# Attention scores and values as three fp32r passes, with the small work of the attention stages put in another order

## The chip, the cores and the metric

The program runs on one core of one Trainium2 chip. The metric is the device time in microseconds (us), the median of three runs. Five engines of the core take part, each with its own queue of instructions that it works off in order: TensorE (PE in the profile), VectorE (DVE), ScalarE (ACT), GpSimd (POOL) and SyncE (SP), which here only starts DMAs. They meet by semaphores: an instruction waits until a counter has reached a number.

## The reference

One layer of a hybrid decoder for 1024 prompt tokens (`x_prompt`) and 32 sample tokens (8 sequences of 4). All three branches read one normed input through one matrix of 4608 columns:

```python
h = _rmsnorm(x, norm_g)
proj = jnp.einsum('btd,de->bte', h, w_in)
qa, ka, va, ga, xb, gb, qc, kc, vc, gc = jnp.split(proj, SPLIT_IDX, axis=-1)
...
qc = _rmsnorm(qc.reshape(B, T, SWA_HEADS, SWA_HEAD_DIM), q_g)
kc = _rmsnorm(kc.reshape(B, T, SWA_KV_HEADS, SWA_HEAD_DIM), k_g)
...
mixed = jnp.concatenate([oa * jax.nn.silu(ga), ob * jax.nn.silu(gb), oc * jax.nn.silu(gc)], axis=-1)
y = x + jnp.einsum('bte,ed->btd', mixed, w_out)
```

`oa` is a retention, `ob` a gated linear recurrence, `oc` the attention that the change touches: 4 query heads of 128 on 2 key/value heads, a window of 128 keys, so that each block of 128 queries reads its own and the previous block of keys:

```python
s = jnp.einsum('bnqhgd,bnkhd->bnhgqk', q.astype(f32), k.astype(f32)) * (SWA_HEAD_DIM ** -0.5)
s = s - slopes[...] * dist
s = jnp.where(valid[None, :, None, None], s, NEG_INF)
m = jnp.maximum(jnp.max(s, axis=-1, keepdims=True), sink)
p = jnp.exp(s - m)
denom = jnp.sum(p, axis=-1, keepdims=True) + jnp.exp(sink - m)
o = jnp.einsum('bnhgqk,bnkhd->bnqhgd', p / denom, v.astype(f32))
```

## The kernel before

The input projection is cut into 18 units of 256 columns, worked off in the order of `UNITS`. Its products are made in three passes of the type fp32r (`three_pass`, lines 447 to 449): each operand is split into a high part, rounded to fp32r (by ACT), and a low part, the rest (by DVE), and PE multiplies low by high, high by low and high by high. The attention's own products, scores and values, are plain fp32: PE's records hold two for each such matmul.

Units 12 and 14 are `kvC` (keys and values of the first and the second key/value head, called half 0 and half 1), units 13 and 15 `qC` (the two query heads on it), 16 and 17 `gA` (gates). In `kvC` and `qC` a unit has nine groups: eight tiles of 128 tokens (24 passes of 256 columns each on PE) and a ninth for the 32 sample tokens, on which PE spends nothing there: these rows are projected ahead, by `sample_rows`, when the next unit takes them too. Groups of `gA` have 24 passes of 352 columns.

The order of the work is written out by hand. Every engine runs the same program of units and groups. PE does a group in two halves and after each half the *side work* of a half-step s (after the first half of group j it is s = 2j, after the second 2j+1). ACT and DVE do the side work of 2j, then the group's own work, then the side work of 2j+1. `att_slot` maps unit and half-step to the half-step of the attention (unit 13: s, unit 14: s + 18, and so on for half 1), and `att_side` of each engine lists what is done there. For tile t of queries:

- unit 13: PE projects group t, ACT squares and sums it (`q_stat`, line 1045), POOL takes the root (line 1710), DVE scales q (`q_norm`, line 1503)
- half-step 2t+3: PE transposes q (`att_q`, line 680), ACT copies it to `qT` (`q_copy`, line 1067)
- 2t+4: PE makes the scores (line 691), DVE adds the bias and takes the maximum (`att_max`, lines 1531 and 1537); 2t+5: ACT takes the exponentials (`att_exp`, line 1075)
- 2t+6: DVE divides (`att_probs`, lines 1545 and 1547); 2t+8: PE transposes the probabilities (line 704), ACT copies them to `pT` (line 1087)
- 2t+12: PE multiplies by the values (line 714), DVE by the gate (`att_mix`, line 1555)

In `kvC` the same goes for k: `k_stat` (lines 1023 and 1025), `k_norm` (1487), `turn_k` (670), `k_copy` (1032); and ACT copies the sample rows of the next unit out of PSUM (`hold_copy`, line 906). Beside it all ACT and DVE split the next unit's weights (`w_hi`, line 861; `w_low`, line 1249), in `kvC` and `qC` at half-steps 3, 5, 7 and 9 (DVE one later). `SILU_AT` places eight silu rows of 1056 columns on ACT (line 889).

Of the kernel before, what the change touches and what calls it, by code (L numbers as in the profile page):

```python
# [68 lines left out]
def done(g):  # L69
    return sum(UNITS[u][0] not in TOKEN_MAJOR or j < NT for u, j in GROUPS[:g + 1])  # L70

# [34 lines left out]
def layer(nc, io):  # L106
    gammas = [float(1.0 - 2.0 ** (-5.0 - h)) for h in range(H)]
    with ExitStack() as ctx:
# [97 lines left out]
        with ExitStack() as r:  # L206
            sb("mixed_c", [P, 3 * H, TOK], scope=r)
            kT = sb("kT", [P, 2, TOK], scope=r)
            v_c = sb("v_c", [P, 2, NT + 1, DH], scope=r)
# [3 lines left out]
            qT = sb("qT", [P, 2, 2 * P], scope=r)  # L213
            pr = sb("pr", [P, 2, 2, 2 * P + 1], scope=r)
            pT = sb("pT", [P, 2, 4 * P], scope=r)
            cache = sb("cache", [P, DB, DH], scope=r)
            kcT = sb("kcT", [P, DB, P], scope=r)
            tail_rows = pT[0:36, 0, :]
            p_sel = kcT[:, 0:2, :].rearrange("p a n -> p (a n)")
        with ExitStack() as r:  # L220
# [23 lines left out]
            k_ss k_pow kn_set kT_done kT_set q_ss q_pow qn_half qn_set qT_done qT_set  # L244
            sc_done biased sink_set mx_set ex_set pr_set pT_done pT_set av_done mix_c
# [36 lines left out]
        def _(sp):  # L282
# [81 lines left out]
            for half in range(2):  # L364
# [7 lines left out]
                for t in (NT - 1, NT):  # L372
                    n9 = 9 * half + t
                    sp.wait_ge(S_["kn_set"], n9 + 1)
                    if t < NT:
                        store(io["p_k"][:, half], kn[:, n9 % 2, :], "stored_kv")
                        store(io["p_v"][:, half], v_c[:, half, t, :], "stored_kv")
                        continue
                    for b in range(DB):
                        rows = slice(b * DS, (b + 1) * DS)  # L380
                        store(io["s_k"][b, WINDOW - DS:WINDOW, half], kn[rows, n9 % 2, :], "stored_kv")
                        store(io["s_v"][b, WINDOW - DS:WINDOW, half], v_c[rows, half, t, :], "stored_kv")
# [37 lines left out]
        SILU_AT = {(7, 3): 0, (7, 4): 1, (10, 4): 2, (10, 5): 3, (12, 4): 4, (12, 5): 5, (12, 6): 6, (12, 7): 7}  # L420
# [4 lines left out]
        def att_slot(u, s):  # L425

            if u in (13, 15):
# [3 lines left out]
            if u == 16:  # L431
                return 1, s + 18
            if u == 17 and s < 6:
                return 1, s + 30
# [9 lines left out]
        def _(pe):  # L444
# [214 lines left out]
            def turn_k(n9):  # L659
# [4 lines left out]
                if n9 > 0:  # L664
                    pe.wait_ge(S_["kT_set"], n9)
                    if n9 >= 9:
                        pe.wait_ge(S_["qT_set"], 9)
                else:
# [3 lines left out]
            def att_q(n9):  # L672
# [3 lines left out]
                pe.wait_ge(S_["kT_set"], 9 * (n9 // 9) + 9)  # L676
                if n9 > 0:
                    pe.wait_ge(S_["qT_set"], n9)
                for g in range(2):
# [4 lines left out]
            def att_scores(half, t):  # L684
                n8 = 8 * half + t
                pe.wait_ge(S_["qT_set"], 9 * half + t + 1)
                if n8 > 0:
                    pe.wait_ge(S_["biased"], n8)
                for g in range(2):
                    lo = P if t == 0 else 0  # L690
                    mm = pe.matmul(bb[1][:, g * 2 * P + lo:(g + 1) * 2 * P],  # L691
                                   qT[:, (9 * half + t) % 2, g * P:(g + 1) * P],
                                   kT[:, half, (t - 1) * P + lo:(t + 1) * P], start=(g == 0), stop=True,
                                   skip_group_check=True)
                mm.then_inc(S_["sc_done"], 1)

            def att_turn(half, t):
                n8 = 8 * half + t
                pe.wait_ge(S_["pr_set"], n8 + 1)
                if n8 > 0:  # L700
                    pe.wait_ge(S_["pT_set"], n8)
                for kt in range(1 if t == 0 else 0, 2):
# [5 lines left out]
            def att_values(half, t):  # L708
                n8 = 8 * half + t
                pe.wait_ge(S_["pT_set"], n8 + 1)  # L710
                if n8 > 0:
                    pe.wait_ge(S_["mix_c"], n8)
                for kt in range(1 if t == 0 else 0, 2):
                    mm = pe.matmul(bb[3][:, 0:2 * P], v_c[:, half, t - 1 + kt, :],  # L714
                                   pT[:, n8 % 2, kt * 2 * P:(kt + 1) * 2 * P], start=(kt == 0 or t == 0),
                                   stop=(kt == 1))
                mm.then_inc(S_["av_done"], 1)

            def samp_scores(half):
# [4 lines left out]
                for e in range(2):  # L724
                    for c in range(4):
                        b = 2 * c + e
                        q = qT[:, (9 * half + NT) % 2, NS * b:NS * b + NS]
                        pe.matmul(bb[4][32 * c:32 * c + 32, 0:P], q, kcT[:, b, :], start=(e == 0), stop=(e == 1),
                                  skip_group_check=True)
                for e in range(2):  # L730
                    for c in range(4):
                        b = 2 * c + e
                        q = qT[:, (9 * half + NT) % 2, NS * b:NS * b + NS]
                        mm = pe.matmul(bb[4][32 * c:32 * c + 32, P:P + NS], q, kT[:, half, SEQ:TOK], start=False,
# [8 lines left out]
            def samp_values(half):  # L743
# [7 lines left out]
                for c in range(4):  # L751
                    mm = pe.matmul(bb[4][32 * c:32 * c + 32, 2 * P:3 * P], kcT[0:NS, 4, 32 * c:32 * c + 32],
                                   v_c[0:NS, half, NT, :], start=False, stop=True, skip_group_check=True)
# [6 lines left out]
            def att_side(half, s):  # L760
                if s % 2 == 1 and 0 <= (s - 3) // 2 <= NT and s >= 3:
                    att_q(9 * half + (s - 3) // 2)
                if s % 2 == 0 and 0 <= (s - 12) // 2 < NT:
                    att_values(half, (s - 12) // 2)
# [86 lines left out]
        def _(act):  # L851
# [157 lines left out]
            def k_stat(u, j):  # L1009
# [10 lines left out]
                if j == NT:  # L1020
# [4 lines left out]
                act.activation(v_c[0:n, half, j, :], bank[0:n, DH:2 * DH], ACT.Copy,  # L1025
                               scale=rcol[0:n, j:j + 1]).then_inc(S_["k_ss"], 1)

            def k_copy(n9):
# [3 lines left out]
                act.activation(kT[:, half, chunk_cols(t)], bb[0][:, 0:n], ACT.Copy).then_inc(S_["kT_set"], 1)  # L1032
# [16 lines left out]
            def q_copy(n9):  # L1049
                n = tile_rows(n9 % 9)  # L1050
                act.wait_ge(S_["qT_done"], n9 + 1)
                if n9 >= 2:
                    h2, t2 = divmod(n9 - 2, 9)
                    if t2 < NT:
                        act.wait_ge(S_["sc_done"], 8 * h2 + t2 + 1)
                    else:
                        act.wait_ge(S_["ss_done"], h2 + 1)
                if n9 % 9 == NT:
                    act.wait_ge(S_["q_zero"], n9 // 9 + 1)
                    q = qT[:, n9 % 2, :].rearrange("p (c x) -> p c x", c=4)  # L1060
# [6 lines left out]
                act.activation(qT[:, n9 % 2, 0:2 * n], bb[0][:, 0:2 * n], ACT.Copy).then_inc(S_["qT_set"], 1)  # L1067
# [11 lines left out]
            def att_pcopy(half, t):  # L1079
# [4 lines left out]
                if n8 >= 2:  # L1084
                    act.wait_ge(S_["av_done"], n8 - 1)
                lo = 2 * P if t == 0 else 0
                act.activation(pT[:, n8 % 2, lo:], bb[2][:, lo:], ACT.Copy).then_inc(S_["pT_set"], 1)
# [21 lines left out]
            def att_side(half, s):  # L1109
# [4 lines left out]
                if s % 2 == 1 and 0 <= (s - 5) // 2 < NT:  # L1114
                    att_exp(half, (s - 5) // 2)
# [121 lines left out]
        def _(dve):  # L1237
# [236 lines left out]
            def k_norm(u, j):  # L1474
# [9 lines left out]
                if j == NT:  # L1484
                    dve.wait_ge(S_["held"], TOKEN_UNITS.index(u) + 1)
                bank = hold if j == NT else proj_bank(g)
                dve.scalar_tensor_tensor(out=kn[0:n, n9 % 2, :], in0=bank[0:n, 0:DH],
                                         scalar=stat[0:n, 16 + n9 % 2:17 + n9 % 2], in1=gain[0:n, 1, :],
                                         op0=ALU.mult, op1=ALU.mult).then_inc(S_["kn_set"], 1)

# [78 lines left out]
            def samp_qzero(half):  # L1569
                dve.wait_ge(S_["sc_done"], 8 * half + 7)  # L1570
                dve.memset(qT[:, (9 * half + NT) % 2, :], 0.0).then_inc(S_["q_zero"], 1)
# [16 lines left out]
            def att_side(half, s):  # L1588
                if s % 2 == 0 and 0 <= (s - 6) // 2 < NT:
                    att_probs(half, (s - 6) // 2)  # L1590
                if s % 2 == 0 and 0 <= (s - 12) // 2 < NT:
# [3 lines left out]
                if s == 17:  # L1595
                    samp_qzero(half)
                if s == 22:
# [6 lines left out]
            def side(u, s):  # L1604
# [40 lines left out]
                if (u, s) in LRU_AT["scan"]:  # L1645
                    lru_scan(LRU_AT["scan"][u, s])
                if att_slot(u, s):
# [14 lines left out]
            for u in range(1, NU):  # L1662
                for j in range(n_groups(u)):
# [3 lines left out]
                    if UNITS[u][0] == "qC":  # L1667
                        q_norm(u, j)
# [244 lines left out]
```

## Time and profile before

| what | value |
|---|---|
| median of 3 runs | 671.33 us (671.24 to 672.15) |
| the profiled execution | 672.29 us, its span 670.2 us |
| PE busy | 664.5 us, 99% of the span |
| DVE, ACT, POOL busy | 300.2, 288.5, 89.0 us |
| granted TensorE clock | 1.000 |

The span runs from the first to the last instruction; the profiled execution's own time holds 2.1 us more. A matmul's record covers its way through the array and overlaps with its neighbours', so the time that a matmul costs is the distance from its start to that of the next, and not its mean duration. Half 0's attention lies in 373 to 429 us of the span (units 13 and 14), half 1's in 444 to 504 us (units 15 and 16).

### The profile page before, as it was taken

Reading aid. Unit: us, or ns where it says so; the run is one execution under the profiler, and the core shown is the slowest. Engines: PE = TensorE matmul, PEld = TensorE weight load, DVE = VectorE, ACT = ScalarE, POOL = GpSimd, SP = SyncE. Lnnn points to the kernel's source line nnn. Section 1 sums busy time; section 2 is a strip of 40 time slices with the busy share of each in tenths; the row PEclk is TensorE's granted clock in tenths of the full one; section 3 lists DMA queues with packets and bytes.
Section 4 is the critical chain, followed back from the end, with each engine's and each line's share of the span. In section 5 each row is a group of like instructions: output and inputs, shape, how many; then the busy total and the mean of one; then the engine's idle time right before and its main releaser. Section 6 shows DMA issues by size and latency. Waiting matters only on the chain.

```text
span 670.2 us, 12606 instructions
## 1 busy us (share of the span) xinstructions
PE 664.5 (99%) x5030; PEld 646.9 (97%) x5030; DVE 300.2 (45%) x665; ACT 288.5 (43%) x711; POOL 89.0 (13%) x206
## 2 busy tenths in 40 slices
PE   9999999999999999999999999999999999999998
PEld 9999999999999999999999999999899999999998
DVE  6311453443545668695442465237542870400000
ACT  7473343323233377799635555345543460200000
POOL 0001141424342000000003321222100000000000
PEclk9999999999999999999999999999999999999999
DMA  9913105131312301101040202131002551522220
GB/s 347 383 36 96 64 1 202 52 99 33 99 33 72 106 1 63 64 1 64 1 152 2 79 1 80 38 100 64 1 1 74 158 179 34 160 66 66 66 66 32
DMA packets 28149, 54.19 MB, mean 81 GB/s; under 512 B 2520, under 2 KB 20696, under 8 KB 25884
## 3 DMA queue, kind: packets, MB, share of 16 engines
q1 hardware_dynamic: 27804, 52.85, 23.6%
q8 instruction: 40, 0.66, 0.4%
q10 hardware_dynamic: 288, 0.54, 0.2%
q14 instruction: 17, 0.14, 0.1%
HBM read 46.30 MB, written 9.12 MB: 83 GB/s over the span
## 4 chain that ended last, share of the span: by engine, by line
PE 97%; DMA 1%; ACT 1%; issue 1%; POOL 0%; DVE 0%; DVEq 0%; SPq 0%; POOLq 0%
PE proj L447 22%; PE proj L449 21%; PE proj L448 21%; PE branch L449 4%; PE branch L448 4%; PE branch L447 4%; PE branch L714 2%; PE branch L691 2%; PE branch L558 1%; PE branch L575 1%; PE branch L646 1%; PE branch L592 1%; DMA lead<-w_units 1%; PE proj L492 1%; PE proj L497 1%; PE proj L500 1%
## 5 line engine op out<-in xcount | busy, mean ns | idle before, releaser
L447 PE MATMUL proj<-big 128*128 128x352 f32 (+1 forms) x912 | 289.8, 318 | 0.0
L449 PE MATMUL proj<-big 128*128 128x352 f32 (+1 forms) x912 | 277.9, 305 | 0.0
L448 PE MATMUL proj<-big 128*128 128x352 f32 (+1 forms) x912 | 277.9, 305 | 0.0
L447 PEld LDWEIGHTS proj<-big 128*128 128x128 f32 x912 | 171.7, 188 | 5.2 <-issue 3.3
L448 PEld LDWEIGHTS proj<-big 128*128 128x128 f32 x912 | 171.8, 188 | 0.2
L449 PEld LDWEIGHTS proj<-big 128*128 128x128 f32 x912 | 171.8, 188 | 0.0
L1249 DVE TENSOR_TENSOR big<-lead,big 128x512 fp32r<-128x512 f32 (+1 forms) x72 | 48.9, 690 | 54.9 <-ACT big L861 54.9
L449 PE MATMUL branch<-m_hi,big 128*128 128x352 f32 x180 | 58.0, 322 | 0.0
L448 PE MATMUL branch<-m_lo,big 128*128 128x352 f32 x180 | 58.0, 322 | 0.0
L447 PE MATMUL branch<-m_hi,big 128*128 128x352 f32 x180 | 57.9, 322 | 0.0
L1709 POOL TENSOR_SCALAR stat<-stat 128x1 f32<-128x1 f32 (+2 forms) x68 | 18.2, 267 | 282.7 <-ACT junk L1023 176.7
L861 ACT ACTIVATE big<-lead 128x512 fp32r<-128x512 f32 (+1 forms) x72 | 44.5, 627 | 5.0 <-DMA lead<-w_units 3.6
L1332 DVE SCALAR_TENSOR_TENSOR sT<-branch,stat,cr 128x128 f32<-128x128 f32 (+1 forms) x36 | 12.2, 339 | 65.5 <-PE branch L558 51.2
L1710 POOL TENSOR_TENSOR stat<-stat 128x1 f32<-128x1 f32 (+2 forms) x68 | 40.2, 591 | 5.7
L1692 DVE TENSOR_TENSOR xy<-branch,xy 128x352 f32<-128x352 f32 x15 | 7.9, 524 | 61.6 <-PE branch L449 59.7
L449 PE MATMUL proj<-m_hi,big 128*128 128x352 f32 x108 | 34.8, 322 | 0.0
L448 PE MATMUL proj<-m_lo,big 128*128 128x352 f32 x108 | 34.8, 322 | 0.0
L447 PE MATMUL proj<-m_hi,big 128*128 128x352 f32 x108 | 34.7, 322 | 0.0
L447 PEld LDWEIGHTS branch<-m_hi,big 128*128 128x128 f32 x180 | 33.8, 188 | 0.0
L449 PEld LDWEIGHTS branch<-m_hi,big 128*128 128x128 f32 x180 | 33.8, 188 | 0.0
L448 PEld LDWEIGHTS branch<-m_lo,big 128*128 128x128 f32 x180 | 33.8, 188 | 0.0
L957 ACT ACTIVATE o_nrm<-branch,stat 128x128 f32<-128x128 f32 x32 | 11.8, 369 | 38.6 <-DVE mixed L1381 26.9
(246 smaller groups left out, 953.0 us busy)
## 6 DMA issues: line engine op xcount, KB each, us to landing
lead<-w_units SPq DMA_DIRECT2D x17, 1024.0 KB, 5.0
xy<-x_T SPq DMA_DIRECT2D x24, 176.0 KB, 2.5
out_y_T<-xy SPq DMA_DIRECT2D x24, 176.0 KB, 1.9
lead<-w_out SPq DMA_DIRECT2D x6, 512.0 KB, 4.6
xy<-w_out SPq DMA_DIRECT2D x6, 512.0 KB, 3.7
mixed<-x_T SPq DMA_DIRECT2D x8, 352.0 KB, 7.5
mixed<-x_prompt SPq DMA_DIRECT2D x5, 512.0 KB, 14.4
s<-state_ret SPq DMA_DIRECT2D x4, 512.0 KB, 4.0
```

The costliest lines, as they stand in the source:

```text
L447: pe.matmul(out, a_lo, b_hi, start=first, stop=False)
L448: pe.matmul(out, a_hi, b_lo, start=False, stop=False)
L449: return pe.matmul(out, a_hi, b_hi, start=False, stop=last)
L691: mm = pe.matmul(bb[1][:, g * 2 * P + lo:(g + 1) * 2 * P], qT[:, (9 * half + t) % 2, g * P:(g + 1) * P], kT[:, half, (t - 1) * P + lo:(t + ...
L714: mm = pe.matmul(bb[3][:, 0:2 * P], v_c[:, half, t - 1 + kt, :], pT[:, n8 % 2, kt * 2 * P:(kt + 1) * 2 * P], start=(kt == 0 or t == 0), st ...
L861: act.activation(w_part(u % 2, 0)[:, cols], raw[:, cols], ACT.Copy).then_inc(S_["w_hi_set"], 1)
L957: act.activation(o_nrm[:, m % 2, :], bb[1 + m % 2][:, 0:P], ACT.Copy, scale=stat[:, 8 + m % 2:9 + m % 2]).then_inc(S_["o_set"], 1)
L1249: dve.tensor_tensor(w_part(u % 2, 1)[:, cols], raw[:, cols], w_part(u % 2, 0)[:, cols].bitcast(F32), ALU.subtract).then_inc(S_["w_lo_set"], 1)
L1332: dve.scalar_tensor_tensor(out=sT[0:n, m % 2, 0:n], in0=bb[0][0:n, 0:n], scalar=rcol[0:n, c:c + 1], in1=mask, op0=ALU.mult, op1=ALU.mult). ...
L1692: dve.tensor_tensor(y_out[:, g % 3, :], y_banks[f][:, 0:CH], x_res[:, g % 3, :], ALU.add).then_inc(S_["y_set"], 1)
L1709: link(pool.tensor_scalar(ss, ss, 1.0 / DH, ecol[0:n, t:t + 1], ALU.mult, ALU.add))
L1710: return pool.tensor_tensor(rs, ss, neghalf[0:n, 0:w], ALU.pow)
```

## The change

1. Scores and values are made in three fp32r passes. `kT`, `qT`, `pT` and `v_c` get the type fp32r and hold a high and a low part instead of two buffers; ACT's copies write the high part, and DVE writes the low part with new instructions: `k_low` and `q_low` (a subtraction from PSUM of 128 and 256 columns), `p_low` (512 columns) and one of 128 columns for v in `k_norm`. PE waits for these too. The transposes stay fp32.
2. The sample rows keep fp32 copies of their own (`kT_s`, `q_s`, `v_raw`); v of the last prompt tile is copied twice, once plain for the output.
3. DVE's `q_norm` of tile t moves from unit 13's own work into `att_side`, half-step 2t+2, behind the division of tile t-2.
4. ACT's exponentials move from half-step 2t+5 to 2t+4. In the stream of ACT they stand ahead of the squares of tile t+2.
5. Values and `att_mix` come one group earlier (2t+10).
6. Four silus move from half-steps 4 to 7 of unit 12 to 10, 12, 14 and 16.
7. In half 1 everything from attention half-step 17 on comes half a group later.

```diff
@@ att_slot, SILU_AT @@
-        SILU_AT = {(7, 3): 0, (7, 4): 1, (10, 4): 2, (10, 5): 3, (12, 4): 4, (12, 5): 5, (12, 6): 6, (12, 7): 7}
+        SILU_AT = {(7, 3): 0, (7, 4): 1, (10, 4): 2, (10, 5): 3, (12, 10): 4, (12, 12): 5, (12, 14): 6, (12, 16): 7}
-            if u in (13, 15):
+            if u == 13 or u == 15 and s < 17:
                 return (u - 13) // 2, s
...
             if u == 16:
-                return 1, s + 18
+                return 1, s + 17
@@ PE @@
             def att_scores(half, t):
                 pe.wait_ge(S_["qT_set"], 9 * half + t + 1)
+                pe.wait_ge(S_["qT_low"], n8 + 1)
...
-                    mm = pe.matmul(bb[1][:, g * 2 * P + lo:(g + 1) * 2 * P],
-                                   qT[:, (9 * half + t) % 2, g * P:(g + 1) * P],
-                                   kT[:, half, (t - 1) * P + lo:(t + 1) * P], start=(g == 0), stop=True,
-                                   skip_group_check=True)
+                    for i, (a, b) in enumerate(((1, 0), (0, 1), (0, 0))):
+                        mm = pe.matmul(bb[1][:, g * 2 * P + lo:(g + 1) * 2 * P], qT[:, a, g * P:(g + 1) * P],
+                                       kT[:, b, (t - 1) * P + lo:(t + 1) * P], start=(g == 0 and i == 0),
+                                       stop=(i == 2), skip_group_check=True)
             def att_values(half, t):
                 pe.wait_ge(S_["pT_set"], n8 + 1)
+                pe.wait_ge(S_["pT_low"], n8 + 1)
+                pe.wait_ge(S_["v_low"], n8 + 1)
...
-                    mm = pe.matmul(bb[3][:, 0:2 * P], v_c[:, half, t - 1 + kt, :],
...
+                    mm = three_pass(bb[3][:, 0:2 * P], v_c[:, 0, t - 1 + kt, :], v_c[:, 1, t - 1 + kt, :], p[0], p[1],
+                                    kt == 0 or t == 0, kt == 1)
@@ ACT, att_side @@
                 if s % 2 == 0 and 0 <= (s - 8) // 2 < NT:
                     att_pcopy(half, (s - 8) // 2)
                 if s % 2 == 0 and s >= 2 and (s - 2) // 2 <= NT:
                     q_copy(9 * half + (s - 2) // 2)
-                if s % 2 == 1 and 0 <= (s - 5) // 2 < NT:
-                    att_exp(half, (s - 5) // 2)
+                if s % 2 == 0 and 0 <= (s - 4) // 2 < NT:
+                    att_exp(half, (s - 4) // 2)
@@ DVE @@
+            def q_low(n9):
+                dve.wait_ge(S_["qT_set"], n9 + 1)
+                dve.tensor_tensor(qT[:, 1, :], bb[0][:, 0:2 * P], qT[:, 0, :].bitcast(F32),
+                                  ALU.subtract).then_inc(S_["qT_low"], 1)
...
             def att_side(half, s):
                 if s % 2 == 0 and 0 <= (s - 6) // 2 < NT:
                     att_probs(half, (s - 6) // 2)
-                if s % 2 == 0 and 0 <= (s - 12) // 2 < NT:
-                    att_mix(half, (s - 12) // 2)
+                if s % 2 == 0 and 0 <= (s - 2) // 2 <= NT:
+                    q_norm(13 + 2 * half, (s - 2) // 2)
+                if s % 2 == 0 and 0 <= (s - 10) // 2 < NT:
+                    att_mix(half, (s - 10) // 2)
                 if s % 2 == 0 and 0 <= (s - 4) // 2 < NT:
                     att_max(half, (s - 4) // 2)
...
+                if s % 2 == 0 and 0 <= (s - 8) // 2 < NT:
+                    p_low(half, (s - 8) // 2)
+                if s % 2 == 0 and 0 <= (s - 2) // 2 < NT:
+                    q_low(9 * half + (s - 2) // 2)
@@ DVE, the loop over units @@
-                    if UNITS[u][0] == "qC":
-                        q_norm(u, j)
```

The order on DVE in the middle of unit 13, two tiles before the change (`qn` is the scaled q, `stat` the row sums and their inverses, `pr` the scores and then the probabilities, `mixed` the gated output):

```order
L1503 SCALAR_TENSOR_TENSOR qn<-proj,stat,gain 128x128 x2
L1545 RECIPROCAL stat<-stat 128x2
L1547 TENSOR_SCALAR pr<-pr,stat 128x256 x2
L1555 TENSOR_TENSOR mixed<-branch,mixed 128x2x128
L1531 SCALAR_TENSOR_TENSOR pr<-branch,cc 128x2x256
L1537 TENSOR_REDUCE stat<-pr 128x2
L1503 SCALAR_TENSOR_TENSOR qn<-proj,stat,gain 128x128 x2
L1545 RECIPROCAL stat<-stat 128x2
```

The same place after the change, where the scaling of q stands between division and maximum, and two low parts follow:

```order
L1601 RECIPROCAL stat<-stat 128x2
L1603 TENSOR_SCALAR pr<-pr,stat 128x256 x2
L1559 SCALAR_TENSOR_TENSOR qn<-proj,stat,gain 128x128 x2
L1611 TENSOR_TENSOR mixed<-branch,mixed 128x2x128
L1587 SCALAR_TENSOR_TENSOR pr<-branch,cc 128x2x256
L1593 TENSOR_REDUCE stat<-pr 128x2
L1544 TENSOR_TENSOR pT<-branch,pT 128x512
L1537 TENSOR_TENSOR qT<-branch,qT 128x256
L1601 RECIPROCAL stat<-stat 128x2
```

What moved: the norm of a tile stood behind the maximum of the tile two earlier, and now the maximum stands behind the norm of the tile one later.

The order on ACT there before the change (`junk` takes the squares of q, `pr` the exponentials, `pT` and `qT` are the copies out of PSUM):

```order
L1087 ACTIVATE pT<-branch 128x512
L1067 ACTIVATE qT<-branch 128x256
L1045 ACTIVATE junk,stat<-proj 128x128 x2
L1075 ACTIVATE pr,stat<-pr,stat 128x257 x2
L1087 ACTIVATE pT<-branch 128x512
```

And on ACT after the change, from its first exponentials in unit 13 on, with the load of their table ahead (`big` is the high part of the next unit's weights):

```order
L1106 ACT_TABLE_LOAD
L1106 ACTIVATE pr,stat<-pr,stat 128x129 x2
L1078 ACTIVATE junk,stat<-proj 128x128 x2
L880 ACTIVATE big<-lead 128x512
L1098 ACTIVATE qT<-branch 128x256
L1106 ACTIVATE pr,stat<-pr,stat 128x257 x2
L1078 ACTIVATE junk,stat<-proj 128x128 x2
L880 ACTIVATE big<-lead 128x512
L1118 ACTIVATE pT<-branch 128x256
```

What moved: exponentials and table load stood behind the squares and now stand ahead of them, so that the squares wait for what the exponentials wait for.

## Rows read from the trace of the kernel before

**Rows 1.** Waits on PE: line, whom it waited for, us in total, times, longest.
```profile
PE branch L670 <- ACT kT L1032: 1.0, 1, 1.0
PE branch L680 <- DVE qn L1503: 0.6, 1, 0.6
```
**Rows 2.** Groups by line, shapes kept apart: records, busy us, mean ns, idle before.
```profile
L714 PE MATMUL branch<-pT,v_c 128*128 128x256 f32 x60 | 15.6, 380 | 0.0
L691 PE MATMUL branch<-kT,qT 128*128 128x256 f32 x56 | 14.4, 378 | 0.0
```
**Rows 3.** The chain that ended last, in order of time: start us, us, what.
```profile
375.76 0.44 PE branch L691 x4
...
394.96 0.22 PE branch L680 x2
...
396.62 0.86 PE branch L714 x4
397.48 0.86 PE branch L691 x4
398.35 0.44 PE branch L704 x4
...
400.22 0.22 PE branch L680 x2
```
**Rows 4.** Timeline of PE: start us, us, instruction. Transposes of q, tiles 1, 5 and 8.
```profile
377.48 0.38 PE L680 MATMUL branch<-ident,qn 128*128 128x128 f32 x2
...
394.81 0.38 PE L680 MATMUL branch<-ident,qn 128*128 128x128 f32 x2
...
409.01 0.31 PE L680 MATMUL branch<-ident,qn 32*128 32x32 f32 x2
```
**Rows 5.** Timeline of ACT, tile 5: start us, us, instruction, idle before.
```profile
395.22 0.39 ACT L1067 ACTIVATE qT<-branch 128x256 f32<-128x256 f32 x1 [1.05 <-PE branch L680]
395.50 0.27 ACT L1045 ACTIVATE junk<-proj 128x128 f32<-128x128 f32 x1
...
396.00 0.52 ACT L1075 ACTIVATE pr<-pr,stat 128x257 f32<-128x257 f32 x1
```
**Rows 6.** Timeline of DVE, the same stretch.
```profile
397.31 0.61 DVE L1503 SCALAR_TENSOR_TENSOR qn<-proj,stat,gain 128x128 f32<-128x128 f32 x2 [1.83 <-POOL stat L1710]
397.83 0.16 DVE L1545 RECIPROCAL stat<-stat 128x2 f32<-128x2 f32 x1
...
398.55 0.42 DVE L1555 TENSOR_TENSOR mixed<-branch,mixed 128x256 f32<-128x256 f32 x1
398.90 0.69 DVE L1531 SCALAR_TENSOR_TENSOR pr<-branch,cc 128x512 f32<-128x512 f32 x1
399.62 0.69 DVE L1537 TENSOR_REDUCE stat<-pr 128x2 f32<-128x514 f32 x1
```
**Rows 7.** Timeline of ACT at the first exponentials; of DVE, a low part of the weights.
```profile
378.68 0.64 ACT L861 ACTIVATE big<-lead 128x512 fp32r<-128x512 f32 x1
379.33 1.28 ACT L1075 ACT_TABLE_LOAD   x1
380.63 0.41 ACT L1075 ACTIVATE pr<-pr,stat 128x129 f32<-128x129 f32 x1
...
388.65 0.68 DVE L1249 TENSOR_TENSOR big<-lead,big 128x512 fp32r<-128x512 f32 x1
389.25 0.16 DVE L1545 RECIPROCAL stat<-stat 128x2 f32<-128x2 f32 x1
```
**Rows 8.** Timeline of ACT and PE in units 12 and 13: a silu, then the last k tiles.
```profile
350.48 1.09 ACT L889 ACTIVATE mixed<-mixed 128x1056 f32<-128x1056 f32 x1
...
366.86 0.36 ACT L1025 ACTIVATE v_c<-proj,stat 128x128 f32<-128x128 f32 x1
...
370.26 0.28 ACT L1032 ACTIVATE kT<-branch 128x128 f32<-128x128 f32 x1
...
370.81 0.24 PE L670 MATMUL branch<-ident,kn 32*128 32x32 f32 x1
```

More of the change, by code:

```diff
@@ L381, in _ @@
                         store(io["s_k"][b, WINDOW - DS:WINDOW, half], kn[rows, n9 % 2, :], "stored_kv")
-                        store(io["s_v"][b, WINDOW - DS:WINDOW, half], v_c[rows, half, t, :], "stored_kv")
+                        store(io["s_v"][b, WINDOW - DS:WINDOW, half], v_raw[rows, 1, :], "stored_kv")
                 load_w(15 + 2 * half)
@@ L732, in samp_scores @@
                         b = 2 * c + e
-                        q = qT[:, (9 * half + NT) % 2, NS * b:NS * b + NS]
-                        mm = pe.matmul(bb[4][32 * c:32 * c + 32, P:P + NS], q, kT[:, half, SEQ:TOK], start=False,
+                        q = q_s[:, NS * b:NS * b + NS]
+                        mm = pe.matmul(bb[4][32 * c:32 * c + 32, P:P + NS], q, kT_s[:, half, :], start=False,
                                        stop=(e == 1), skip_group_check=True)
@@ L752, in samp_values @@
                     mm = pe.matmul(bb[4][32 * c:32 * c + 32, 2 * P:3 * P], kcT[0:NS, 4, 32 * c:32 * c + 32],
-                                   v_c[0:NS, half, NT, :], start=False, stop=True, skip_group_check=True)
+                                   v_raw[0:NS, 1, :], start=False, stop=True, skip_group_check=True)
                 mm.then_inc(S_["sav_done"], 1)
@@ L1024, in k_stat @@
                                accum_out=stat[0:n, 12 + n9 % 2:13 + n9 % 2]).then_inc(S_["k_ss"], 1)
-                act.activation(v_c[0:n, half, j, :], bank[0:n, DH:2 * DH], ACT.Copy,
-                               scale=rcol[0:n, j:j + 1]).then_inc(S_["k_ss"], 1)
+                if half == 1 and j < NT:
+                    act.wait_ge(S_["av_done"], min(j + 2, NT))
+                if half == 1 and j == NT - 1:
+                    act.wait_ge(S_["stored_kv"], 16 * (2 + 2 * DB))
+                if half == 1 and j == NT:
+                    act.wait_ge(S_["sav_done"], 1)
+                if j >= NT - 1:
+                    act.activation(v_raw[0:n, j - NT + 1, :], bank[0:n, DH:2 * DH], ACT.Copy,
+                                   scale=rcol[0:n, j:j + 1]).then_inc(
+                                   S_["v_kept" if j < NT else "k_ss"], 1)
+                if j < NT:
+                    act.activation(v_c[:, 0, j, :], bank[:, DH:2 * DH], ACT.Copy, scale=rcol[:, j:j + 1]).then_inc(
+                        S_["k_ss"], 1)
             def k_copy(n9):
@@ L1031, in k_copy @@
                 act.wait_ge(S_["kT_done"], n9 + 1)
-                act.activation(kT[:, half, chunk_cols(t)], bb[0][:, 0:n], ACT.Copy).then_inc(S_["kT_set"], 1)
+                if half == 1 and t < NT:
+                    act.wait_ge(S_["sc_done"], NT)
+                out = kT[:, 0, chunk_cols(t)] if t < NT else kT_s[:, half, :]
+                act.activation(out, bb[0][:, 0:n], ACT.Copy).then_inc(S_["kT_set"], 1)
             def q_stat(u, j):
```

91 lines of the change are left out of this document (62 added, 29 removed).

## The prediction

> **What bounds the kernel now.** I read the busy times first: PE is busy for 664.5 of 670.2 us, at a granted clock of 1.000, so only two things move the end: work that PE has more or less of, and new gaps on PE. The waits of PE come next: after its first instructions it waits twice, 1.0 us for a copy of k on ACT and 0.6 us for a scaled q from DVE [rows 1]. Everything else on DVE, ACT and POOL lies beside PE's passes. Then the groups by line, for the work that the change replaces: 60 records of the values and 56 of the scores [rows 2], two for each fp32 matmul of 256 columns, so 30 and 28 matmuls; four more of the scores have 128 columns. Last, the chain and the timelines of one tile in the middle of unit 13, on which the forecast rests: what does a tile cost PE, and how long do ACT, POOL and DVE take to hand it the next q?
>
> **A tile on PE, before and after.** In rows 3 the transposes of q start 5.26 us apart. They cost 0.22; the twelve passes between 395.18 and 396.62 take 1.44, so a pass of 256 columns takes 0.12, and 24 of them 2.88; values and scores 0.86 each, 0.43 a matmul; the transposes of the probabilities 0.44. Three passes cost 0.36 instead of 0.43: 0.07 less on each of 58 matmuls, 4.1 us in all. The first scores of each half have 128 columns. Their two fp32 matmuls cost 0.44 [rows 3]; no row shows an fp32r pass of 128 columns. The ends are 0.06 for a pass (half of the 256-column pass) and 0.22 (a whole fp32 matmul of that width), so six passes cost 0.36 to 1.32; I take 0.11, what a transpose of 128 columns costs: 0.66, and 0.2 more in each half. Work on PE falls by 4.1 - 0.4 = 3.7 us. A full tile then costs 2.88 + 0.72 + 0.72 + 0.44 + 0.22 = 4.98.
>
> The trace shows two fp32 records of 0.215 for what fp32r does in one of 0.12. The Trainium skill (FP8 and Floating Point Precision, TensorE Precision Notes) says that true fp32 takes four passes through the array; three for four would save a quarter of 0.43, 0.11, and 6.2 us in all instead of 4.1. The trace agrees only in part: its fp32r pass costs more than a quarter of 0.43.
>
> **The new loop.** Before, DVE made the maximum of tile v-2 ahead of the norm of q of tile v, and ACT squared tile v ahead of the exponentials of v-2, so neither held the other. After, by the order on both engines: the norm of q of tile v-1, then the gate's product, then bias and maximum of v-2 on DVE; ACT waits for it with the exponentials of v-2, and the squares of tile v stand behind these; POOL's root and the norm of q of tile v follow. That closes a loop from norm to norm, once for each tile:
>
> - two norms 0.52 (397.31 to 397.83), gate 0.35, bias 0.72 (398.90 to 399.62), maximum 0.69 plus 0.04 to ACT [rows 6]
> - exponentials 1.00 (two of 0.52, the second close on the first) [rows 5]
> - start of the squares to start of the norm 1.81 (395.50 to 397.31) [rows 5, 6]
>
> Sum 5.13 us, against 4.98 on PE. And while DVE still owes the next unit's low parts, q's norm of tiles 2, 3 and 4 stands behind more: squares 0.50, high part 0.65 (378.68 to 379.33), low part 0.60 (388.65 to 389.25), division 0.72 (397.83 to 398.55) replace the 1.81 [rows 5 to 7], without the gate: 0.52 + 0.72 + 0.73 + 1.00 + 0.50 + 0.65 + 0.60 + 0.72 = 5.44. PE's own work is shorter there, since values and transposes have hardly begun.
>
> Where PE stalls, from one transposes of q to the next (due: two half groups 2.88, transposes 0.22, and the side work that is there):
>
> - Tile 2: due 2.88 + 0.72 + 0.22 = 3.82. From PE's start to ACT's copy 0.41 (394.81 to 395.22), copy 0.28, two short exponentials of 0.41, then 0.50 + 0.65 + 0.60 + 0.72, norm to PE 0.67: 4.65 in half 1, stall 0.8. In half 0 the load of the table, 1.28, now stands ahead of the squares: 5.93, stall 2.1 [rows 4, 5, 7].
> - Tile 3: due 4.04, loop 5.44, stall 1.4. Tile 4: due 4.62, stall 0.8. In both halves.
> - Tile 5: the values of tile 1 wait for their low part. Behind the start of q's norm on DVE come 0.52 + 0.35 + 0.72 + 0.69, and the low part of p. A subtraction of 512 columns from PSUM is in no row; bias (0.69) and the weights' low part (0.68) are nearest, and I take 0.72 with its signal, bounds 0.55 and 0.8. That is 3.0 after the norm's start, 2.35 after PE's transposes of q, where PE is ready at 0.22 + 1.44 = 1.66. Stall 0.7.
> - Tiles 5 to 7, half 0: three rounds of the loop are 15.4. PE is due after 4.98 twice and then 3.1, since the ninth group leaves it only 1.03 of the next unit's sample rows beside 2.1 of side work: 13.1, stall 2.3 with the 0.7 above. Then tile 8 again 0.7 for the low part, and some 0.4 for two later ones. Half 0: 2.1 + 1.4 + 0.8 + 2.3 + 0.7 + 0.4 = 7.7, with 0.2 for scores waiting on the low part of q 7.9. As a check, the spacing of tiles 1 to 8 before is 31.5 us [rows 4]; after it would be about 38.
> - Half 1: 0.8 + 1.4 + 0.8 + 0.7 + 0.2 for tiles 2 to 6. In the ninth group PE has nothing, values of tile 3 come 0.22 after q's transposes, and their low part 2.35 after them at the latest: 1.6, since DVE is half a us ahead by then. The half-step that is moved puts a half group of `gA` ahead of the next transposes, which covers that wait and the 0.6 of before. With 0.2 for scores: 5.7, less 0.6.
>
> **Keys.** Without the silus in half-steps 4 to 7 ACT copies k in time, and the wait of 1.0 goes [rows 1]. The first three moved silus fall in ACT's idle time: a group of k takes PE 3.0 us (24 passes and a transpose) and ACT about 0.8 (squares 0.27, v 0.25, k 0.28), and a silu takes 1.0; only the first, with a table load of 1.28 ahead of it, fills the 2.2 that are left. The fourth stands ahead of the sample rows' squares, where ACT is in a hurry: squares, root, the last norm of k, the copy of the next unit's sample rows, then the copy of k at 370.26, and PE takes it at 370.81 [rows 8]. One silu (1.0 apart, 1.09 long) and the second copy of v (0.25, the distance of such copies of 0.36) shift 370.26 to 371.5; copy 0.28 and the new low part of k, 0.35 as the norm of k, give 372.2. Stall 1.4. Half 1 has no silu there: 0.4.
>
> **At nothing.** The low part of v, 0.27 ahead of the norm of k: turns of k are 0.7 or more later. About 29 us of new work on DVE (16 each of 0.35, 0.35, 0.42 and 0.68), which is busy 300 of 670: only its places count, above. The single buffers of q, p and v: their readers are a group ahead. SP issues the same DMAs. The later end of half 1: it ends well inside unit 17, where PE waits for nothing; if that cover failed, half a group would be the price, 12 x 0.12 x 352/256 = 2.0.
>
> **Sum.** -3.7 + 7.9 + 5.7 - 0.6 + 1.4 + 0.4 - 1.0 = +10.1 us. The profiled execution would go from 672.3 to 682.4. It lies 1.0 above the median of 671.3, so the forecast is 671.3 + 10.1 = 681.4.
>
> **Rivals.**
> - *The loop does not bind and PE only saves:* -3.7 - 1.0 - 0.6 and 0.4 for k: 666.4, faster. The place is the norm of q in unit 13. It decides at 4.98 for the full tile and 4.0 for tiles 2 to 4. For it: 5.13 is only 0.15 over, and DVE could gain that much. Against: tiles 3 and 4 lack 1.4 and 0.8, each from rows. 0.10.
> - *Only the beginnings cost:* tiles 2 to 4 (4.3 and 3.0) and the keys, while the steady loop runs under PE: -3.7 - 1.6 + 7.3 + 1.8 = +3.8, 675.1. For it: the small margins of tiles 5 to 8. Against: the group that is missing on PE at tile 7. 0.12.
> - *More than forecast:* passes of 128 columns at 0.22 (+1.3), low parts of 0.8, more waits for low parts in unit 14 (+2): 685 to 687. 0.08.
> - *The clock falls in the stalls.* The granted clock stayed at 1.000 through a wait of 1.0; my longest is 2.1. A full tile at 1.2 instead of 2.4 GHz would cost 5 us more, so 686 for one. 0.03. The Trainium skill (TensorE: Matmul & The Clock Gate, HAM oscillation) has TensorE throttled again after idle gaps; no row here shows it.
>
> The forecast keeps 0.67, with its own range 678.5 to 684.5. 8 in 10 lie in 674 to 686. About 0.2% is what a measurement of this kernel can tell from no change, 1.3 us: faster 0.10, within it 0.03, slower 0.87.
>
> **What would show it.** Right: PE waits on the transposes of q for DVE's norm, longest about 2 at tile 2 of half 0, over 1 at tile 3 in both halves; waits on the values' passes of 0.2 to 1.6 for the low part of p; one of about 1.4 on the transposes of k between units 12 and 13; values at 0.72 a tile; the norms of q 5.1 apart at tiles 5 to 7, with the maximum directly ahead of the exponentials and these ahead of the squares. Wrong: PE busy without gaps in unit 13; norms spaced like PE's work; gaps at the start of units 16 and 17 instead.

## The result and the profile after

| | before | after |
|---|---|---|
| median of 4 runs each | 671.29 us | 681.39 us |
| ratio, 95% interval | | 1.0145, 1.0133 to 1.0157 |
| profiled execution, its span | 672.29 us, 670.2 us | 681.47 us, 679.3 us |
| PE, DVE, ACT busy | 664.5, 300.2, 288.5 us | 663.7, 322.3, 288.9 us |

The change makes the kernel 10.1 us slower at the median and 9.2 in the profiled executions. The forecast was 681.4. One execution each of e8_two_after (3643 us) and e9_two_all (795 us) took far longer than the others of its kernel, for a reason that no run shows, and stands in no number below. The page of after, shares of the busy engines and of the chain that ended last:

```profile
PE 663.7 (98%) x5092; PEld 647.4 (95%) x5092; DVE 322.3 (47%) x729; ACT 288.9 (43%) x713; POOL 89.2 (13%) x206
...
PE 38%; DVE 3%; ACT 3%; issue 1%; POOL 1%; DVEq 0%; ACTq 0%
```

DVE's 22 us of new work are no loss by themselves, with DVE busy less than half of the span; but DVE, ACT and POOL now stand on the chain with 7% of the span together. Before, PE had 97% and DVE 0%; the chain of after is followed back over only half of the span. PE's waits, in the columns of [rows 1]: the two single waits of before are gone, and these are there.

```profile
PE branch L695 <- DVE qn L1559: 6.8, 7, 2.0
PE branch L458 <- issue: 3.3, 5, 1.6
PE branch L683 <- DVE kT L1532: 1.1, 1, 1.1
...
PE branch L683 <- issue: 0.3, 1, 0.3
```

L695 is the transposes of q, L458 here the first pass of the values, L683 the transposes of k. The profile writes "issue" where it sees no releaser. For the values what they wait for is the low part of p: in half 0 DVE starts it at 395.81 and it takes 0.68, and PE starts the values at 396.59. Groups by line, what answers to [rows 2]: three records per product of 256 columns.

```profile
L708 PE MATMUL branch<-kT,qT 128*128 128x256 f32 x84 | 12.4, 284 | 0.0
L458 PE MATMUL branch<-pT,v_c 128*128 128x256 f32 x30 | 9.1, 305 | 3.3 <-issue 3.3
```

The transposes of q, which answer to [rows 4], on PE's timeline:

```profile
377.48 0.38 PE L695 MATMUL branch<-ident,qn 128*128 128x128 f32 x2
383.40 0.43 PE L695 MATMUL branch<-ident,qn 128*128 128x128 f32 x2 [1.97 <-DVE qn L1559]
388.85 0.44 PE L695 MATMUL branch<-ident,qn 128*128 128x128 f32 x2 [1.17 <-DVE qn L1559]
394.29 0.44 PE L695 MATMUL branch<-ident,qn 128*128 128x128 f32 x2 [0.58 <-DVE qn L1559]
396.59 0.36 PE L458 MATMUL branch<-pT,v_c 128*128 128x256 f32 x1 [0.43 <-issue]
399.96 0.38 PE L695 MATMUL branch<-ident,qn 128*128 128x128 f32 x2
```

From tile 1 on the distances are 5.92, 5.45, 5.44 and 5.67; forecast were 5.93, 5.44, 5.44 and about 5.7. Tiles 1 to 8 take 38.1 (377.48 to 415.61), where they took 31.5.

The chain that ended last, tiles 4 and 5 of half 0 (start, us, what), goes once round the loop without touching PE:

```profile
393.64 0.60 DVE qn L1559 x2
394.24 0.33 DVE mixed L1611
394.57 0.61 DVE pr L1587
...
395.20 0.70 DVE stat L1593
...
396.34 0.68 ACT pr L1106 x3
397.02 0.52 ACT junk L1078 x4
...
397.63 0.38 POOL stat L1773
...
398.08 0.69 POOL stat L1774
...
399.08 0.34 DVE qn L1559
```

That is the norm of q of tile 4, the gate, bias and maximum of tile 3, its exponentials, then the squares, the root and the norm of tile 5. The squares start at 396.92, right behind the exponentials, where in [rows 5] they stood ahead of them. In the same stretch PE waits twice and is not on the chain at all.

### The profile page after: what moved, and what is told of

Read it like the earlier page. It is cut to its first block and busy times, and to the rows that moved or that the text cites. A ratio compares the mean times of both kernels' runs of the same rounds, so it can differ in the third digit from the quotient of the medians.

```text
span 679.3 us, 12851 instructions
## 1 busy us (share of the span) xinstructions
PE 663.7 (98%) x5092; PEld 647.4 (95%) x5092; DVE 322.3 (47%) x729; ACT 288.9 (43%) x713; POOL 89.2 (13%) x206
## 5 line engine op out<-in xcount | busy, mean ns | idle before, releaser
L458 PE MATMUL proj<-big 128*128 128x352 f32 (+1 forms) x912 | 288.8, 317 | 0.0
L458 PEld LDWEIGHTS proj<-big 128*128 128x128 f32 x912 | 171.9, 188 | 5.0 <-issue 3.3
L458 PE MATMUL branch<-m_hi,big 128*128 128x352 f32 x180 | 58.0, 322 | 0.0
L1363 DVE SCALAR_TENSOR_TENSOR sT<-branch,stat,cr 128x128 f32<-128x128 f32 (+1 forms) x36 | 12.2, 338 | 65.5 <-PE branch L569 51.2
L458 PE MATMUL proj<-m_hi,big 128*128 128x352 f32 x108 | 34.8, 322 | 0.0
L458 PEld LDWEIGHTS branch<-m_hi,big 128*128 128x128 f32 x180 | 33.8, 188 | 0.0
```

Source lines behind the costliest of these rows:

```text
L458: pe.matmul(out, a_lo, b_hi, start=first, stop=False)
L1363: dve.scalar_tensor_tensor(out=sT[0:n, m % 2, 0:n], in0=bb[0][0:n, 0:n], scalar=rcol[0:n, c:c + 1], in1=mask, op0=ALU.mult, op1=ALU.mult). ...
```

## The experiments

Each ratio is to the kernel before, on the same chip.

### e1_exp_late: the exponentials back behind the squares

```diff
-                if s % 2 == 0 and 0 <= (s - 4) // 2 < NT:
-                    att_exp(half, (s - 4) // 2)
+                if s % 2 == 1 and 0 <= (s - 5) // 2 < NT:
+                    att_exp(half, (s - 5) // 2)
```

> The changed kernel with item 4 alone taken back: the exponentials stand at half-step 2t+5 again, behind the squares of tile t+2. **Theory (the closed loop):** the squares no longer wait for the maximum, so the loop from norm to norm opens; what is left is norm, gate, bias, maximum, exponentials and division, 0.52 + 0.34 + 1.45 + 1.10 + 0.73 = 4.1 us against 4.98 on PE. The waits of PE for the norm of q (6.8 us) and most of those for the low part of p (3.3) go; a table load in front of a copy (about 1.6 in half 0) and some of 0.3 to 0.9 for low parts remain, 5 us in all. About 672.7 us, 8.7 under the changed kernel, and the norms of q follow PE. **Rival (low parts):** the new instructions of DVE are what lengthens a tile, wherever the exponentials stand: 679 or more. **Rival (DVE's place is the cause, not ACT's):** the norm ahead of the maximum holds it up all the same: 677 to 681.

Measured: 673.12 us, ratio 1.0023 (1.0014 to 1.0032). PE's waits:

```profile
PE branch L695 <- DVE qn L1559: 1.6, 2, 1.4
PE branch L458 <- issue: 1.2, 2, 0.8
```

One half-step on ACT is worth 8.3 of the 10.1 us, 0.4 off the theory's 672.7, with all low parts in place. Both rivals fall: the norm still stands ahead of the maximum on DVE, and it holds nothing up. The waits for q's norm fall from 6.8 to 1.6, of which 1.4 is tile 2 of half 0, where the table load stands in front. The loop needs the early exponentials; without them the norm's early place costs nothing.

### e2_norm_back: the norm back, the exponentials early

```diff
@@ att_side, DVE @@
-                if s % 2 == 0 and 0 <= (s - 2) // 2 <= NT:
-                    q_norm(13 + 2 * half, (s - 2) // 2)
@@ DVE, the unit's own work @@
+                    if UNITS[u][0] == "qC":
+                        q_norm(u, j)
```

> The changed kernel with item 3 alone taken back: DVE scales q in the unit's own work, behind the maximum of the tile two earlier, while the exponentials stay ahead of ACT's squares. **Theory (the closed loop):** the loop stays closed and grows by what now stands between exponentials and norm on DVE: the maximum of a tile waits for scores that wait for this norm, and squares behind the exponentials: 0.52 + 0.73 + 0.34 + 1.45 + 1.00 + 1.81 = 5.9 us a tile instead of 5.1 to 5.2. About 689.7 us, 8 slower than the changed kernel. **Rival (the norm's early place is the cause):** taking it back gives the time back: 672 to 676. **Rival (low parts):** no change from 681.4.

Measured: 690.86 us, ratio 1.0287 (1.0271 to 1.0303), 9.5 slower than the changed kernel. PE's waits:

```profile
PE branch L458 <- issue: 8.6, 8, 2.2
PE branch L458 <- DVE pT L1544: 3.5, 2, 1.8
PE branch L695 <- DVE qn L1559: 3.0, 4, 1.4
PE branch L708 <- DVE qT L1537: 2.0, 2, 1.0
```

The norm's early place is a help and not the harm. The exponentials ahead of the squares close a loop in either order of DVE; with the norm late it is longer. DVE's timeline, the norms of tiles 3, 5 and 6:

```profile
387.91 0.61 DVE L1559 SCALAR_TENSOR_TENSOR qn<-proj,stat,gain 128x128 f32<-128x128 f32 x2 [2.49 <-POOL stat L1774]
...
400.39 0.61 DVE L1559 SCALAR_TENSOR_TENSOR qn<-proj,stat,gain 128x128 f32<-128x128 f32 x2 [1.89 <-POOL stat L1774]
406.20 0.61 DVE L1559 SCALAR_TENSOR_TENSOR qn<-proj,stat,gain 128x128 f32<-128x128 f32 x2 [1.89 <-POOL stat L1774]
```

From tile 2 on the distances are 5.9, 6.1, 6.4 and 5.8, where 5.9 was expected; what makes the 6.1 and 6.4 is not taken apart here. DVE stands idle for POOL's root each time, and its low parts come later, so most of PE's waits are now at values and scores. Of the time over 689.7, 1.2 us, the clock accounts for all and more: it cost 1.6 in the profiled execution (last section).

### e3_both_back: both moves back, the rest stays

The two edits above together.

> The changed kernel with items 3 and 4 both taken back: norm and exponentials stand where they stood before, the three fp32r passes with their low parts, the earlier values and the moved silus stay. **Theory (the closed loop):** no loop; PE saves 3.7 us of work, and loses about 7 on a late copy at the table load, on low parts of q and p and on keys: about 674 us, 7.4 under the changed kernel. **Rival (low parts):** 680 or more. **Rival (PE's work was sized wrong, the passes save nothing):** 677 to 678 with the same waits.

Measured: 673.65 us, ratio 1.0028 (1.0017 to 1.0038). PE's waits are 2.8 for values, 1.1 and 0.5 for k, 1.4 for the scores' low part of q, and 0.4 on weights:

```profile
PE branch L458 <- issue: 2.8, 4, 1.1
```

It lies 0.5 above e1_exp_late, so the norm's move by itself gains 0.5 at most (the intervals of the two ratios overlap, and the profiled spans are 671.6 and 671.5): it trades a wait for the low part of q against one for q's norm. The rest of the change, without either move, is 2.2 us slower than the kernel before: its waits for low parts and keys outweigh what PE saves.

### e4_order_fp32: the two moves alone, on the kernel before

The edits of items 3 and 4 on the kernel before, in fp32, with nothing else changed.

> The kernel before with items 3 and 4 alone: fp32 scores and values, no low parts, silus and values where they were, but the norm of q behind the division and the exponentials ahead of the squares. **Theory (the closed loop):** the two moves alone make the waits: the same loop of 5.1 us (5.4 at tiles 2 to 4) against 5.26 on PE for a full tile, so the full tiles lose little and the beginnings and the ninth group the most: about 6.2 + 5.9 us of waits on PE for the norm, 682.6 us in all. **Rival (low parts):** without them there is no loss: 671 to 673. **Rival (only together):** half of it, 676 to 678.

Measured: 683.72 us (682.31 to 684.47), ratio 1.0176 (1.0161 to 1.0191). PE's waits in attention are all for q's norm:

```profile
PE branch L680 <- DVE qn L1503: 9.7, 8, 2.4
```

No low part exists here, and the loss is 12.2 us. In the profiled execution 1.6 of it is the clock's (last section), which covers the 1.1 over the theory and leaves 10.6 for the waits. The two moves make the whole of the loss; the rest of the change takes back 2.3 (681.4 against 683.7), of which those 1.6 may be a part, as the profile of the changed kernel has no such stretch.

### e5_silu, e6_table: the two single terms

```diff
@@ e5_silu @@
-... (12, 10): 4, (12, 12): 5, (12, 14): 6, (12, 16): 7}
+... (12, 8): 4, (12, 10): 5, (12, 12): 6, (12, 14): 7}
@@ e6_table, ACT, behind the half-step's work @@
+                if (u, s) == (13, 2):
+                    act.activation(stat[:, 18:19], ones[:, 0:1], ACT.Exp)
```

> The changed kernel with the four moved silus one group earlier (half-steps 8, 10, 12 and 14 of unit 12), so that none stands ahead of the sample rows' squares. **Theory (the fourth silu holds up the last copy of k):** the wait of PE for the low part of k between units 12 and 13, 1.15 us, falls to 0.3 as between units 14 and 15, which has no silu: 680.3, 1.1 under the changed kernel. **Rival (the low part itself is what is late):** the wait stays at 1.0 or more, 681.4. **Rival (the time is given back at the waits for q):** the wait goes, but DVE and ACT, already behind, reach the norm of tile 2 no earlier: 681 to 681.5.

Measured: 680.68 us, ratio 1.0135 (1.0121 to 1.0149), 0.7 under the changed kernel's median; its span is 678.5 against 679.3. The last transposes of k in unit 12, and those of q of tile 2:

```profile
369.61 0.22 PE L683 MATMUL branch<-ident,kn 32*128 32x32 f32 x1 [0.28 <-DVE kT L1532]
...
382.37 0.44 PE L695 MATMUL branch<-ident,qn 128*128 128x128 f32 x2 [1.97 <-DVE qn L1559]
```

The wait fell from 1.15 to 0.28 and both rows stand 1.03 earlier than in the changed kernel. So the silus' place was the cause of that wait. All four were moved here; only the fourth had stood ahead of the squares of the sample rows. In half 1 PE's wait for k grew from 0.3 to 0.5, which fits a gain of 0.7 to 0.8 instead of 1.1.

> The changed kernel with one exponential of a single column added on ACT in half-step 2 of unit 13, so that the table is loaded there and not at the first real exponentials; its result is not used. **Theory:** the load of 1.28 us leaves the chain copy, exponentials, squares, weights, root, norm at tile 2, and lies where ACT would have waited for PE's half group; the wait of PE there falls from 2.0 to 0.7: 680.1, 1.3 under the changed kernel. **Rival (the loop catches up):** tile 3 waits for the loop from the maximum of tile 1, not for tile 2's start, and takes back what tile 2 gave: 681.4. **Rival (the early load delays q's squares of tile 1):** a new wait at tile 1, 681.5 to 682.5.

Measured: 680.18 us, ratio 1.0132 (1.0116 to 1.0147), 1.2 under the changed kernel. Tiles 2 and 3:

```profile
382.13 0.44 PE L695 MATMUL branch<-ident,qn 128*128 128x128 f32 x2 [0.55 <-DVE qn L1561]
387.58 0.44 PE L695 MATMUL branch<-ident,qn 128*128 128x128 f32 x2 [1.15 <-DVE qn L1561]
```

The wait at tile 2 fell by 1.4 and tile 3 still follows 5.45 later with its 1.15: a loop passes on what its start gains. The table load was worth 1.3, as in the forecast's 2.1 against 0.8 for the two halves.

### e7_all: open loop, silus earlier, table early

The three edits together.

> Three edits on the changed kernel: the exponentials late again (as in e1_exp_late), the silus one group earlier, and the early load of the table. **Theory:** with the loop open, 673.1 was measured; the table load no longer makes PE wait 1.4 for the norm of tile 2 in half 0, and the keys' wait of 1.2 falls to 0.3 or less: 673.1 - 1.4 - 0.9 = 670.8, 0.7 under the kernel before; waits of 0.4 to 0.8 for low parts of p remain. **Rival (waits move on):** as tile 2 is earlier, PE waits at tile 3 or for the low part of q, as in e3_both_back (0.9): 671.5 to 673. Right would be a gain of 2 us or more over e1_exp_late.

Measured: 670.92 us (11 runs, 670.78 to 671.54), ratio 0.9990 (0.9981 to 0.9999). The best of the kernels that compute everything: 2.2 under e1_exp_late, 10.5 under the changed kernel, and 0.7 under the kernel before, whose median on this chip was 671.64. The interval ends at 0.9999, so that it is faster at all is barely shown. What is left:

```profile
PE branch L458 <- issue: 1.2, 2, 0.8
...
PE branch L683 <- DVE kT L1534: 0.5, 2, 0.2
...
PE branch L695 <- DVE qn L1561: 0.3, 1, 0.3
```

In a full tile of half 1 the transposes of q stand 4.95 apart (465.84 to 470.79), where they stood 5.26 [rows 3]; the forecast for PE's own work was 4.98.

### e8_two_after, e9_two_all, e10_two_look: two passes for three

```diff
-                    for i, (a, b) in enumerate(((1, 0), (0, 1), (0, 0))):
+                    for i, (a, b) in enumerate(((0, 1), (0, 0))):
...
-                    mm = three_pass(bb[3][:, 0:2 * P], v_c[:, 0, ...], v_c[:, 1, ...], p[0], p[1], ...)
+                    pe.matmul(bb[3][:, 0:2 * P], v_c[:, 0, t - 1 + kt, :], p[1], ...)
+                    mm = pe.matmul(bb[3][:, 0:2 * P], v_c[:, 0, t - 1 + kt, :], p[0], ...)
```

> The changed kernel with two passes in place of three for scores and values: the product with the low part of q, and with the low part of v, is left out; every low part is still made and waited for. PE has 58 passes of 0.12 and 4 of 0.10 less, 7.4 us. **Theory (the closed loop sets the end of the tiles):** in half 0 the norms of q stay 5.4 to 5.2 us apart at tiles 2 to 7, and what PE saves there becomes longer waits; time comes back only where PE was last: before the first wait of each half, and after tile 7. About a third, 2.5 us: 679. **Rival (PE sets the end, and the waits are few and local):** all of it, 674. **Rival (the low parts set the end):** nothing, 681.4.

> The same left out of e7_all, the kernel with the loop open. **Theory:** a full tile has 4.26 us of work on PE, and what ACT, POOL and DVE need from norm to norm is 4.15, so PE stays the bound in the full tiles; only the waits of e7_all at the end of each half and at tiles 2 and 3 grow. Some 4.5 of the 7.4 us come back: 666.5. **Rival (all):** 663.5. **Rival (none, PE is not the bound here either):** 670.9. The distance between this gain and that of the changed kernel is what the loop swallows.

> The kernel of e8_two_after once more, for its profile. 0.8 of 7.4 us came back there instead of 2.5. **Theory (the loop sets the end of the tiles):** the norms of q in half 0 stand 5.4 us apart to tile 4 and 5.2 from tile 5 on, as in the changed kernel, in the last tiles too, with a wait of PE for q's norm or for a low part in every tile. **Rival:** the norms come closer together by 0.5 or more, and the time is lost to something behind unit 14.

Measured: on the changed kernel 680.53 us (e8_two_after, three executions of 680.47 to 680.71) and 678.86 in the single one of e10_two_look, which has the usable profile: 0.9 and 2.5 of the 7.4 us come back, where 2.5 was expected of both. On the open loop 666.49 (e9_two_all, three executions of 666.22 to 666.79), 4.4 back, where 4.5 was expected. Removing the same work from PE is worth 1.7 times as much once the loop is open by e10_two_look, and 5 times by e8_two_after. Why the same kernel differs by 1.7 us between these two is not shown. The clock is a likely part: its mean was 0.995 to 0.997 in e8_two_after and 0.999 to 1.000 in e9_two_all, and a low stretch that meets no later wait costs 1.6 (last section). The norms of q on DVE, without the pass, in e10_two_look:

```profile
382.52 0.60 DVE L1559 SCALAR_TENSOR_TENSOR qn<-proj,stat,gain 128x128 f32<-128x128 f32 x2
387.97 0.60 DVE L1559 SCALAR_TENSOR_TENSOR qn<-proj,stat,gain 128x128 f32<-128x128 f32 x2
393.42 0.60 DVE L1559 SCALAR_TENSOR_TENSOR qn<-proj,stat,gain 128x128 f32<-128x128 f32 x2
398.60 0.61 DVE L1559 SCALAR_TENSOR_TENSOR qn<-proj,stat,gain 128x128 f32<-128x128 f32 x2 [0.94 <-POOL stat L1774]
403.79 0.61 DVE L1559 SCALAR_TENSOR_TENSOR qn<-proj,stat,gain 128x128 f32<-128x128 f32 x2 [0.95 <-POOL stat L1774]
```

5.45, 5.45, 5.18, 5.19. And in the changed kernel, with all three passes:

```profile
382.74 0.60 DVE L1559 SCALAR_TENSOR_TENSOR qn<-proj,stat,gain 128x128 f32<-128x128 f32 x2
388.19 0.60 DVE L1559 SCALAR_TENSOR_TENSOR qn<-proj,stat,gain 128x128 f32<-128x128 f32 x2
...
398.81 0.61 DVE L1559 SCALAR_TENSOR_TENSOR qn<-proj,stat,gain 128x128 f32<-128x128 f32 x2 [0.94 <-POOL stat L1774]
```

The same distances to 0.01 us, from tile 2 to tile 5. This is the most direct evidence: what PE saves changes nothing in the pace of the tiles.

## Why the prediction was right

- **The loop.** Forecast 5.44 at tiles 2 to 4 and 5.13 later; measured 5.45 and 5.17 to 5.19. Its cause was put too widely: the prediction let the two moves close it together, and e2_norm_back shows that the exponentials' move closes one alone, which the norm's move shortens. That it binds is shown by e1_exp_late (opened: 8.3 us back), by e4_order_fp32 (made alone: 12.2 us lost, 1.6 of it by the clock) and by the pass left out of e10_two_look (not moved).
- **The stalls of q and of p's low part.** I measure each on PE as the distance from the start of the last pass to that of the waiting one, less the pass. Half 0: 2.1, 1.3, 0.7 at tiles 2, 3, 4; 0.6, 0.15, 0.6, 0.95 in tiles 5 to 7; 0.6 and 0.2 behind: 7.2, forecast 7.9. Half 1: 0.7, 1.3, 0.7, 0.6, 0.15, and 1.7 for the values of tile 3: 5.2, forecast 5.7. Of the 1.2 too much, 0.4 are the two waits of scores for the low part of q, which never came, and 0.2 the waits behind tile 8; the others are a tenth or less each.
- **Keys.** 1.3 and 0.45 by the same measure, forecast 1.4 and 0.4. e5_silu shows that the silus' place is what made the first. The old wait of k is gone; by distance it had been 1.15 and not 1.0, and that for q 0.8 and not 0.6. But the forecast put that wait down to the silus alone, and it belongs to the one profiled execution of the kernel before. There ACT had first waited for the weights:

```profile
348.37 0.63 ACT L861 ACTIVATE big<-lead 128x512 fp32r<-128x512 f32 x1 [0.73 <-DMA lead<-w_units]
...
353.88 0.30 PE L670 MATMUL branch<-ident,kn 128*128 128x128 f32 x1 [1.00 <-ACT kT L1032]
```

In e4_order_fp32, which has the same silus, that DMA was in time, and the same transposes (at 352.94) come 0.3 late with no idle time shown. The 1.0 that the forecast took off for moving the silus is at most 0.3 in such an execution.
- **PE's work.** A pass of 128 columns costs 0.10, the forecast took 0.11: six lie between 375.39 and 376.01. A full tile costs 4.95, forecast 4.98. The sum does not close entirely: stalls of 7.2 + 5.2 + 1.75 less 1.95 before make 12.2, the span grew by 9.1, so PE gained 3.1 elsewhere and not 3.7. After a wait the first pass of the values is followed by the next 0.19 later and not 0.12 (it is so at 396.59), which explains 0.35; the rest stays open.
- **Sum.** Stalls forecast too large by 1.6 (1.2, and 0.4 in the waits of before), work saved too large by 0.6: the forecast for the profiled execution, 682.4, was 0.9 above its 681.47. That the median came out exactly is partly chance: the profiled execution of before had lain 1.0 above its median, and that of after lay 0.1 above. The late DMA above can be 0.85 of that 1.0. If so, the forecast for the median took off 1.0 that the median never held, and this made up for stalls that it had too large. The new work on DVE, which the forecast put at about 29 us, adds 22 to DVE's busy time; nothing in the sum hung on it.
- **The rivals.** "The loop does not bind" is false here, and its 666.4 was too low even for an open loop: with one, 670.9 is the best that was reached, since waits for low parts and keys remain. "Only the beginnings cost" fails at tiles 5 to 7, which lose 2.3 in half 0 as forecast. The clock rival: below.

## What to carry to other kernels

Before an instruction is moved ahead of another on an in-order queue, write down what each of the two waits for, and follow it across the engines until it comes back: moving work by a single half-step can close a ring, whose length then replaces the work of the busiest engine as the price of a turn, and a second move may lengthen or shorten it. The ring's length is a sum of rows that are all in the trace before the change. And when the bound is such a ring, work saved on the busiest engine is worth little: here passes of 7.4 us in all were worth 0.9 to 2.5 in it and 4.4 outside it.

## What the runs showed of the hardware

**The clock falls after some waits, and this costs 1.6 us or nothing.** In e10_two_look PE waits 2.21 for q at tile 2, starts at 383.18, and a microsecond later the granted clock is 0.50, 1.2 GHz, until about 387.6. Windows of this run (us, PE, PEld, DVE, ACT and POOL busy, granted clock, DMA):

```profile
383.00:384.00 1.00, 0.82 (x7) 0.83 (x8) 0.97 (x3) 0.35 (x1) 0.00 (x0) 1.00 0.00 0
384.00:385.00 1.00, 1.00 (x7) 1.00 (x6) 0.77 (x2) 0.56 (x4) 0.00 (x0) 0.60 0.00 0
385.00:386.00 1.00, 1.00 (x6) 1.00 (x6) 0.00 (x0) 1.00 (x8) 0.00 (x0) 0.50 0.00 0
...
387.00:388.00 1.00, 1.00 (x8) 1.00 (x8) 0.96 (x5) 0.33 (x1) 0.37 (x2) 0.70 0.00 0
388.00:389.00 1.00, 1.00 (x9) 0.88 (x9) 1.00 (x4) 0.00 (x0) 0.00 (x0) 1.00 0.03 8
```

The same came behind the longest waits of e2_norm_back (2.16) and e4_order_fp32 (2.36), and not behind the 1.97 in the profile of the changed kernel or the 1.99 that e10_two_look itself has later. In kind this agrees with the Trainium skill (TensorE: Matmul & The Clock Gate, HAM oscillation), which has TensorE throttled again after idle gaps; the gaps here are shorter than those that it describes. The forecast priced a fall at 5 us. What it costs depends on what follows. In e10_two_look the stretch of 3.4 us met tile 3, where the changed kernel's PE waited 1.17: that wait vanished, and the next norm came no later. In e4_order_fp32 it came behind the last wait of the attention. PE's own work from the waiting transposes of q to the next, with all of it the same and no wait between, in e4_order_fp32 (first two rows) and in the kernel before:

```profile
483.24 0.44 PE L680 MATMUL branch<-ident,qn 128*128 128x128 f32 x2 [2.36 <-DVE qn L1503]
...
491.24 0.31 PE L680 MATMUL branch<-ident,qn 32*128 32x32 f32 x2
...
473.44 0.44 PE L680 MATMUL branch<-ident,qn 128*128 128x128 f32 x2 [0.62 <-DVE qn L1503]
...
479.81 0.31 PE L680 MATMUL branch<-ident,qn 32*128 32x32 f32 x2
```

8.00 us against 6.37: the stretch cost 1.6, and no later wait of PE takes it back. In e2_norm_back it is the same from the values at 489.69 to the next ones at 497.26, 7.57 against 5.98 in the changed kernel. All executions of these two kernels have a mean clock of 0.995 to 0.997. So have two of the changed kernel's four, at 681.31 and 681.88 us, where the two with 0.999 took 681.29 and 681.47; where in the span the clock fell in them is not on record, and in one of the two it cost nothing that can be seen.

**A wait is longer than its idle time.** A pass of 256 columns costs 0.12 and its record lasts 0.28, so the idle time shown starts late. The row at 383.40 shows 1.97 where the distance gives 2.13, and the values at 401.77 wait 0.15 with no idle time shown. Over the attention and the keys the waits of PE add up to 11.5 by idle time and to 14.2 by distance: stalls are better taken from the distance of starts.
